# Down projections and pool mixer: which engine makes the token sums and one group's window average

## The chip, the cores and the metric

The kernel runs on one core of a Trainium2 chip. The metric is the device time of one execution in microseconds. All data are float32. TensorE is called PE, its weight loads PEld, VectorE is DVE, ScalarE is ACT, GpSimd is POOL, and SyncE (SP) issues most of the weight loads. Each engine takes its own instructions in the order in which they were written; semaphores tie the engines together.

## The reference, cut to what matters

Two blocks follow each other, each of depth 2, over 512 tokens and 1024 channels. The change touches the first block: the down projection of the gated feed-forward in both of its layers, and the pool mixer, which is the mixer of its second layer.

```python
def _pool_mixer(h, w_grp, scale):
    hf = h.reshape(Bn, T, POOL_GROUPS, POOL_GROUP)      # 4 groups of 256 channels
    for gi, w in enumerate((2, 4, 8, 16)):
        xg = hf[:, :, gi]
        cs = cumsum(pad(xg, w))                          # over the tokens
        outs.append((cs[:, w:] - cs[:, :T]) / minimum(t + 1, w) - xg)
    y = einsum('btgc,gcd->btgd', stack(outs), w_grp)
    return y.reshape(Bn, T, D) * scale

def _conv_ffn(h, w_up, conv_w, conv_b, w_down):
    u, v = split(h @ w_up)
    uc = conv_b + sum_j shifted(u, j) * conv_w[j]
    return (silu(uc) * v) @ w_down                       # depth 2816, 1024 outputs
...
    x = _layer_norm(ALPHA * x + g1 * y, ...)             # after the mixer
    x = _layer_norm(ALPHA * x + g2 * y, ...)             # after the feed-forward
```

## The kernel before

Data lie with channels on the partitions and tokens along the free dimension. The down projection multiplies `G` (22 depth tiles of 128 channels by 512 tokens) with `w_down`. It uses the seven-product form of a 2 by 2 block product: the two halves of the output channels are one pair, even and odd depth tiles the other, the two halves of the tokens the third. Four of the seven products need sums of weight blocks (**left sums**), four need sums of blocks of `G` (**token sums** or right sums, R[1] to R[4]).

The depth is cut in three groups, h = 0, 1, 2, with 4, 4 and 3 pairs of depth tiles. `DOWN` lists twelve steps (h, q), where q says which two output tiles are made: steps 0 to 3 are group 0, steps 4 and 5 group 1, steps 6 and 7 group 2, steps 8 and 9 group 1 again, steps 10 and 11 group 2. The token sums of a group are made once. A step has four parts on PE (`ffn_down_pe`, matmuls on L905): part 0 needs only the weights and `G`; part 1 is the first to need the left sums of the step and the token sums of the group.

Who does what in a step before the change:

- POOL (`ffn_pool`, `down_left_pool`) makes the left sums of each step, four tensor_tensor instructions (L823, L825, L826, L828), and right behind them issues the DMAs that bring tiles of `ada_rest` into three rotating buffers `ada_late`. The DMA of a tile waits until DVE has used the tile three places before ("ada used"). So the left sums of step it + 1 stand in POOL's queue behind DMAs that wait for DVE.
- DVE (`down_evac_dve`, L958 to L972) adds the seven products from PSUM into `R`, then makes two token sums or one (`down_right_dve`, L853 to L861), then works off the ada tiles of the step (`ada_tile_dve`, L350, or L354 and L357, each 128 x 1024). Four token sums of group 1 come one by one behind steps 0 to 3, those of group 2 in pairs behind steps 4 and 5.
- POOL makes the token sums of group 0 early, in the up projection (`first_right_pool`, L836 to L841).
- ACT copies the first product of a step out of PSUM.

In layer 1 DVE also has the sums of squares of the context behind step 0 and the context's normalisation (L1930) behind step 3. The buffer of R[4] of group 2 shares its place with the context's squares `ctx_sq`.

Behind the down projection of layer 0 comes a layer norm (`shifted_norm_dve`), then the pool mixer. DVE averages the groups of channels one after another (`pooled_dve`): group 0 (window 2) in the norm, then group 3 (window 16), group 2, and group 1 (window 4) last, all through the two buffers `pool_a` and `pool_b`, with the evacuations of finished rows between them (`pool_dve`). PE (`pool_pe`) takes the groups in the order 0, 3, 2, 1, with the matmuls against ones for the next norm between them. POOL has nothing to do there but to clear the pads (`pads_pool`).

Of the kernel before, what the change touches and what calls it, by code (L numbers as in the profile page):

```python
# [13 lines left out]
P = 128  # L14
D = 1024
DT = D // P
T = 512
# [362 lines left out]
def ffn_pool(k, l, first):  # L380

    def issued(until):
        nonlocal first
        last = min(until + LATE, N_ADA[0] + 96)
        late_tiles_pool(k, first, max(first, last))
        first = max(first, last)
    issued(ADA_UP[l][10].stop)
    first_right_pool(k, l)
    issued(ADA_UP[l][FT - 3].stop)
    for it in range(ND):  # L390
        down_left_pool(k, l, it)
        issued(ADA_UP[l][FT - 1].stop if it == 0 else ADA_DOWN[l][it - 1].stop)
    issued(ADA_DOWN[l][-1].stop)


# [445 lines left out]
    g.tensor_tensor(R[4], B[1, 0], R[2], ALU.subtract).then_inc(*k.says(POOL, "down right", l, 0))  # L841


def down_right_dve(k, l, h, j):

    v = k.nc.vector
    B, R = down_right(k, DOWN.index((h, 0)))
    if j == 0:
        if h == 1:
            v.wait_ge(*k.when("products", l, FT - 1, 3))  # L850
        else:
            v.wait_ge(*k.when("down products", l, 3, 3))
        v.tensor_tensor(R[1], B[0, 1], B[0, 0], ALU.subtract).then_inc(*k.says(DVE))  # L853
        v.wait_ge(*k.now(DVE))
    if j == 1:
        v.tensor_tensor(R[2], B[1, 1], R[1], ALU.subtract).then_inc(*k.says(DVE))
    if j == 2:
        v.tensor_tensor(R[3], B[1, 1], B[0, 1], ALU.subtract).then_inc(*k.says(DVE))
        v.wait_ge(*k.now(DVE))
    if j == 3:  # L860
        v.tensor_tensor(R[4], B[1, 0], R[2], ALU.subtract).then_inc(*k.says(DVE, "down right", l, h))  # L861


def ffn_down_pe(k, l):
# [113 lines left out]
def ffn_down_dve(k, l):  # L978
# [5 lines left out]
        v.tensor_tensor(sq[:, 0:2, :], sq[:, 0:2, :], sq[:, 4:6, :], ALU.add).then_inc(*k.says(DVE, st, "squares added"))  # L984
    for it in range(ND):
        down_evac_dve(k, l, it, squares_joined if it == ND - 1 else None)
        if it < 4:
            down_right_dve(k, l, 1, it)
        elif it == 4:
            for j in range(2):  # L990
                down_right_dve(k, l, 2, j)
        elif it == 5:
            for j in range(2, 4):
                down_right_dve(k, l, 2, j)
        if it == 7:
            v.tensor_tensor(sq[:, 0:2, :], R[:, 0:2, :], R[:, 2:4, :], ALU.add).then_inc(*k.says(DVE, st, "half"))
        if it == 8:
# [812 lines left out]
    g.wait_ge(*k.now(POOL))  # L1810


def pool_dve(k):

    v, st, rows = k.nc.vector, ("norm", 1, 0), ROWS["pool"]
    v.wait_ge(*k.when("pads"))
    pg = k.sc[:, 5, :]
    for n in range(DT):
        for g in ((3,), (), (2,), (), (1,), (), (), ())[n]:
            pooled_dve(k, g)  # L1820
        r = rows[n]
        v.wait_ge(*k.when("mm", "pool", 0, n))
        v.wait_ge(*k.when(("norm", 0, 1), "x", r))
        v.scalar_tensor_tensor(k.R[:, r, :], k.ps[:, n % 4, :], pg[:, r:r + 1], k.XA[:, r, :], ALU.mult, ALU.add)\
            .then_inc(*k.says(DVE, "evac", "pool", 0, n))
        if n == 5:
            v.wait_ge(*k.now(DVE))
            v.tensor_tensor(k.pool_a[:, 0, 0:T], k.R[:, 4, :], k.R[:, 5, :], ALU.add).then_inc(*k.says(DVE, "pool sum"))
            v.wait_ge(*k.when(st, "square", 5))
            v.tensor_tensor(k.pool_b[:, 0, 0:T], k.pool_sq[:, 4, :], k.pool_sq[:, 5, :], ALU.add).then_inc(*k.says(DVE, "pool square sum"))  # L1830
    k.mark(DVE, "pool rows")
    norm_scalars_dve(k, 1, 0)
    left_sums_dve(k, 1, 0)
    shifted_norm_dve(k, st)
# [1848 lines left out]
def lay_memory(k):  # L3683
# [59 lines left out]
    k.pool_a, k.pool_b = k.at("pool_a", [P, 2, T + PAD]), k.at("pool_b", [P, 2, T + PAD])  # L3743
    k.pooled = k.at("pooled", [P, DT, T])
    k.pool_sq = k.at("pool_sq", [P, DT, T])

    k.top = block2
    k.AR = [k.at("AR0", [P, 2, NK, 2, CK]), k.at("AR1", [P, 2, NK, 2, CK], xa)]
# [138 lines left out]
def gpsimd_program(k):  # L3887
# [8 lines left out]
        .then_inc(*k.lands("c2_rows_in", "c2 rows"))  # L3896
    ffn_pool(k, 0, N_EARLY)
    pads_pool(k)
    ffn_pool(k, 1, ADA_DOWN[0][-1].stop + LATE)
    rw_consts_pool(k)  # L3900
    end("pre 0")
# [113 lines left out]
```

## Time and profile before

| | |
|---|---|
| median of 3 runs | 2498.15 us (2493.9 to 2502.34) |
| profiled execution | 2495.48 us |
| its span | 2494.1 us, 39647 instructions |
| PE busy | 2334.1 us, 94% of the span |
| DVE busy | 1659.2 us, 67% |
| ACT busy | 640.2 us, 26% |
| POOL busy | 235.9 us, 9% |

The stages that matter here, in us from the span's start: the down projection of layer 0 runs from about 631 to 779, its norm and the pool mixer from 779 to 822, and the down projection of layer 1 from about 1099 to 1250.

A line of the timeline has the start, the length, the engine, the line of the kernel, the operation, what it writes and reads, and how many instructions are merged (xN). In square brackets is the idle time of the engine just before, and what ended it. Only idle time on the path that ends last costs anything.

### The profile page before, as it was taken

How to read it: one execution, taken by the hardware profiler on the slowest of the kernel's cores; microseconds unless marked ns; L12 is line 12 of the kernel's file. 1: busy time of each engine (PE TensorE's matmuls, PEld its weight loads, DVE VectorE, ACT ScalarE, POOL GpSimd, SP SyncE). 2: the span in 40 equal slices, each digit the busy share in tenths (PEclk: the TensorE clock that was granted, in tenths of full speed). 3: DMA queues.
4: the chain of work that ended last, by engine and by line, in shares of the span. 5: the costliest groups of instructions: out<-in, count | busy, mean ns of one | idle time of the engine just before them, and what ended most of it. 6: DMA issues, size and time to landing. Idle time of an engine off the chain costs nothing.

```text
span 2494.1 us, 39647 instructions
## 1 busy us (share of the span) xinstructions
PE 2334.1 (94%) x17066; PEld 1693.8 (68%) x17066; DVE 1659.2 (67%) x2800; ACT 640.2 (26%) x1314; POOL 235.9 (9%) x261
## 2 busy tenths in 40 slices
PE   7988889999997999999999999999997999999997
PEld 3675548888884688888756676676675654546973
DVE  3784378798799888879847879779787123232442
ACT  1323331111002311111043354444444212101111
POOL 2000000020541002024400000000000000000000
PEclk9999999999999999999999999999998999999999
DMA  8232135555432233343221101001010212111102
GB/s 329 90 113 76 60 134 169 172 170 181 161 131 89 85 128 126 135 139 132 95 98 70 40 19 35 21 20 37 3 36 19 85 51 84 51 52 66 35 18 101
DMA packets 42224, 227.99 MB, mean 91 GB/s; under 512 B 4737, under 2 KB 4865, under 8 KB 25793
## 3 DMA queue, kind: packets, MB, share of 16 engines
q1 hardware_dynamic: 21456, 140.56, 15.7%
q0 software_dynamic: 20016, 82.79, 9.8%
q8 instruction: 135, 2.21, 0.4%
q10 hardware_dynamic: 576, 2.11, 0.3%
q14 instruction: 41, 0.33, 0.0%
HBM read 219.14 MB, written 6.29 MB: 90 GB/s over the span
## 4 chain that ended last, share of the span: by engine, by line
PE 84%; DVE 11%; ACT 2%; issue 2%; DMA 1%; POOL 0%; SPq 0%; DVEq 0%; ACTq 0%; POOLq 0%
PE ps L683 20%; PE ps L2283 10%; PE ps L905 8%; PE ps L307 7%; PE ps L3383 3%; PE ps L2064 3%; PE ps L1039 3%; PE ps L455 2%; PE ps L1715 2%; PE ps L3572 2%; PE ps L2293 2%; PE ps L2302 2%; PE ps L3003 1%; PE ps L2971 1%; PE ps L2990 1%
## 5 line engine op out<-in xcount | busy, mean ns | idle before, releaser
L2283 PE MATMUL ps<-H,ring 128*128 128x256 f32 (+1 forms) x832 | 271.4, 487 | 5.4 <-ACT LW L2502 2.6
L683 PE MATMUL ps<-right_sums,left_sums 128*128 128x256 f32 x1056 | 242.8, 379 | 2.7 <-DVE left_sums L663 2.7
L2283 PEld LDWEIGHTS ps<-H,ring 128*128 128x128 f32 x832 | 157.4, 190 | 112.9 <-issue 92.8
L683 PEld LDWEIGHTS ps<-right_sums,left_sums 128*128 128x128 f32 x1056 | 200.5, 190 | 30.6 <-DVE left_sums L663 3.5
L307 PE MATMUL ps<-H,ring 128*128 128x512 f32 (+1 forms) x480 | 181.5, 535 | 0.9 <-DVE ls_tmp L3250 0.9
L683 PE MATMUL ps<-H,ring 128*128 128x256 f32 x704 | 164.2, 385 | 12.7 <-ACT H L626 12.7
L905 PE MATMUL ps<-G,ring 128*128 128x256 f32 x704 | 159.8, 379 | 0.0
L683 PEld LDWEIGHTS ps<-H,ring 128*128 128x128 f32 x704 | 134.6, 192 | 35.6 <-issue 12.8
L307 PEld LDWEIGHTS ps<-H,ring 128*128 128x128 f32 x480 | 91.1, 190 | 88.3 <-issue 84.9
L905 PEld LDWEIGHTS ps<-G,ring 128*128 128x128 f32 x704 | 133.8, 190 | 18.2
L377 POOL DMA_DIRECT2D ada_late<-ada_rest x104 | 56.2, 540 | 684.7 <-DVE mod L357 373.5
L750 ACT ACTIVATE C<-U,params_sb 128x512 f32<-128x512 f32 x44 | 35.9, 816 | 314.9 <-DVE U L775 314.9
L683 PE MATMUL ps<-H,left_sums 128*128 128x256 f32 x352 | 86.9, 388 | 0.0
L3383 PE MATMUL ps<-ring,H 128*128 128x256 f32 x384 | 85.9, 379 | 0.0
L2064 PE MATMUL ps<-O,ring 128*128 128x512 f32 (+1 forms) x256 | 83.6, 486 | 0.6 <-DVE H L2007 0.6
L683 PE MATMUL ps<-right_sums,ring 128*128 128x256 f32 x352 | 83.5, 379 | 0.0
L2007 DVE TENSOR_SCALAR H<-ps,scalars 128x512 f32<-128x512 f32 (+1 forms) x24 | 15.3, 661 | 97.7 <-ACT sq_ctx L2024 61.2
L3383 PEld LDWEIGHTS ps<-ring,H 128*128 128x128 f32 x384 | 72.0, 190 | 12.1 <-issue 3.1
L683 PEld LDWEIGHTS ps<-H,left_sums 128*128 128x128 f32 x352 | 68.2, 194 | 10.8 <-ACT H L626 1.4
L350 DVE CUSTOM_DVE_ANT_0 ada_late<-ada_late,c_row,params_sb 128x1024 f32<-128x1024 f32 x56 | 69.9, 1280 | 6.3 <-DMA ada_late<-ada_rest 6.2
L683 PEld LDWEIGHTS ps<-right_sums,ring 128*128 128x128 f32 x352 | 66.9, 190 | 9.1
L2064 PEld LDWEIGHTS ps<-O,ring 128*128 128x128 f32 x256 | 48.5, 190 | 34.0 <-issue 30.6
(593 smaller groups left out, 4704.2 us busy)
## 6 DMA issues: line engine op xcount, KB each, us to landing
ada_late<-ada_rest POOLq DMA_DIRECT2D x104, 512.0 KB, 3.7
ring<-w_up SPq DMA_DIRECT2D x44, 1024.0 KB, 4.8
ring<-w_down SPq DMA_DIRECT2D x16, 1024.0 KB, 4.9
ring<-od_in SPq DMA_DIRECT2D x16, 1024.0 KB, 4.8
ring<-ev_in SPq DMA_DIRECT2D x15, 1024.0 KB, 4.8
ada_early<-ada_rest POOLq DMA_DIRECT2D x24, 512.0 KB, 4.7
ada_first_sb<-ada_first SPq DMA_DIRECT2D x8, 1024.0 KB, 16.3
ring<-ab_in SPq DMA_DIRECT2D x7, 1024.0 KB, 6.4
```

The lines of the kernel that those rows point to most:

```text
L307: mm = pe.matmul(k.ps[:, (n % deep) * nb + b, 0:tn], wv[:, kk, a * P:(a + 1) * P], rhs[:, kk, t0:t0 + tn], start=(kk == 0), stop=(kk == kt ...
L350: v.tensor_tensor_reduce(w, w, k.c_row[:], 1.0, bias, ALU.mult, ALU.add, k.MOD[part][:, tile, :])\
L377: g.dma_start(k.late[:, j % LATE, :], k.dram["ada_rest"][j]).then_inc(*k.lands(f"late_in{j % LATE}", "ada in", j))
L455: mm = pe.matmul(k.ps[:, n, :], k.W8[:, kk, n * P:(n + 1) * P], k.H[:, kk, 0:T], start=(kk == 0), stop=(kk == DT - 1))
L683: return pe.matmul(product(k, n, j), lhsT[:, i, :], rhs[:, i, :], start=(i == 0), stop=(i == 3))
L905: mm = pe.matmul(product(k, it, j), left[:, i, :], right[:, i, :], start=(i == 0), stop=(i == ni - 1))
L1039: mm = pe.matmul(k.ps[:, bank, :], wv[:, kk, (i % 2) * P:(i % 2 + 1) * P], k.H[:, kk, 0:T], start=(kk == 0), stop=(kk == DT - 1))
L1715: return pe.matmul(out, wv[:, kk, (n % 2) * P:(n % 2 + 1) * P], rhs, start=start, stop=stop)
L2064: mm = k.nc.tensor.matmul(k.ps[:, 2 * (n % 2) + b, 0:tn], wv[:, kk, (n % 2) * P:(n % 2 + 1) * P], k.O[:, kk, t0:t0 + tn], start=(start and ...
L2283: mm = pe.matmul(k.ps[:, bank + b, 0:tn], wv[:, kk, (i % 2) * P:(i % 2 + 1) * P], k.H[:, kk, t0:t0 + tn], start=(kk == 0), stop=(kk == DT ...
L2293: mm = k.nc.tensor.matmul(k.ps[:, bank + n, 0:tn], lhsT, rhs[:, t0:t0 + tn], start=True, stop=True)
L3383: mm = pe.matmul(k.ps[:, 3 + 4 * (u % 2), 0:256], k.H[:, kk, t * P:(t + 1) * P], wv[:, kk, :], start=(kk == 0), stop=(kk == DT - 1))
```

## The change

DVE makes no token sums any more. POOL makes those of groups 1 and 2 too, in pairs: in steps 1 and 2 for group 1, in steps 4 and 5 for group 2. In POOL's queue they stand behind the left sums and the DMAs of the step, and ahead of the left sums of the next step. In layer 1 the first pair of group 2 waits in addition for the context's normalisation. In the pool mixer POOL averages group 1, in two buffers of its own (`pool_four`); it starts when the last tile of the norm is written, and its window average takes a tensor_scalar and a tensor_tensor where DVE used one scalar_tensor_tensor. DVE's `pool_dve` leaves group 1 out.

```diff
@@ ffn_pool
     for it in range(ND):
         down_left_pool(k, l, it)
         issued(ADA_UP[l][FT - 1].stop if it == 0 else ADA_DOWN[l][it - 1].stop)
+        if it in (1, 2):
+            down_right_pool(k, l, 1, it - 1)
+        if it in (4, 5):
+            down_right_pool(k, l, 2, it - 4)
@@
-def down_right_dve(k, l, h, j):
+def down_right_pool(k, l, h, j):
+    g = k.nc.gpsimd
     B, R = down_right(k, DOWN.index((h, 0)))
     if j == 0:
+        g.wait_ge(*k.when("ffn g", l, (7, 15, FT - 1)[h]))
+        g.wait_ge(*(k.when("products", l, FT - 1, 3) if h == 1 else k.when("down products", l, 3, 3)))
+        if h == 2 and l == 1:
+            g.wait_ge(*k.when("context normal", 1))
+        g.tensor_tensor(R[1], B[0, 1], B[0, 0], ALU.subtract).then_inc(*k.says(POOL))
+        g.wait_ge(*k.now(POOL))
+        g.tensor_tensor(R[2], B[1, 1], R[1], ALU.subtract).then_inc(*k.says(POOL))
+    else:
+        g.tensor_tensor(R[3], B[1, 1], B[0, 1], ALU.subtract).then_inc(*k.says(POOL))
+        g.wait_ge(*k.now(POOL))
+        g.tensor_tensor(R[4], B[1, 0], R[2], ALU.subtract).then_inc(*k.says(POOL, "down right", l, h))
@@ ffn_down_dve
         down_evac_dve(k, l, it, squares_joined if it == ND - 1 else None)
-        if it < 4:
-            down_right_dve(k, l, 1, it)
-        elif it == 4:
-            for j in range(2):
-                down_right_dve(k, l, 2, j)
-        elif it == 5:
-            for j in range(2, 4):
-                down_right_dve(k, l, 2, j)
@@
+def pooled_four_pool(k):
+    g, h, (src, dst) = k.nc.gpsimd, k.R[:, pair(1), :], k.pool_four
+    g.wait_ge(*k.when(("norm", 0, 1), "normal", 3))
+    for x in (src, dst):
+        g.memset(x[:, :, 0:PAD], 0.0).then_inc(*k.says(POOL))
+    g.tensor_scalar(src[:, :, PAD:PAD + 1], h[:, :, 0:1], 1.0, None, ALU.mult).then_inc(*k.says(POOL))
+    g.tensor_tensor(src[:, :, PAD + 1:], h[:, :, 1:], h[:, :, 0:T - 1], ALU.add).then_inc(*k.says(POOL))
+    g.wait_ge(*k.now(POOL))
+    g.tensor_tensor(dst[:, :, PAD:], src[:, :, PAD:], src[:, :, PAD - 2:PAD - 2 + T], ALU.add).then_inc(*k.says(POOL))
+    g.wait_ge(*k.now(POOL))
+    fix = k.f("pool_fix", 16, 16).unsqueeze(1).broadcast_to([P, 2, 16])
+    g.tensor_tensor(dst[:, :, PAD:PAD + 16], dst[:, :, PAD:PAD + 16], fix, ALU.mult).then_inc(*k.says(POOL))
+    g.wait_ge(*k.now(POOL))
+    g.tensor_scalar(dst[:, :, PAD:], dst[:, :, PAD:], 1.0 / POOL_WINDOWS[1], None, ALU.mult).then_inc(*k.says(POOL))
+    g.wait_ge(*k.now(POOL))
+    g.tensor_tensor(k.pooled[:, pair(1), :], dst[:, :, PAD:], h, ALU.subtract).then_inc(*k.says(POOL, "pooled", 1))
@@ pool_dve
-        for g in ((3,), (), (2,), (), (1,), (), (), ())[n]:
+        for g in ((3,), (), (2,), (), (), (), (), ())[n]:
             pooled_dve(k, g)
@@ gpsimd_program
     ffn_pool(k, 0, N_EARLY)
     pads_pool(k)
+    pooled_four_pool(k)
     ffn_pool(k, 1, ADA_DOWN[0][-1].stop + LATE)
```

## Rows read from the trace of the kernel before

**Rows 1.** The page: busy time of PE, and the chain's shares by engine.
```profile
PE 2334.1 (94%) x17066; PEld 1693.8 (68%) x17066; DVE 1659.2 (67%) x2800; ACT 640.2 (26%) x1314; POOL 235.9 (9%) x261
...
PE 84%; DVE 11%; ACT 2%; issue 2%; DMA 1%; POOL 0%; SPq 0%; DVEq 0%; ACTq 0%; POOLq 0%
```

**Rows 2.** Busy time in stretches: length, then PE, PEld, DVE, ACT, POOL, clock.
```profile
624.00:779.00 155.00, 149.40 (x671) 126.58 (x669) 130.21 (x202) 14.42 (x28) 71.73 (x69) 1.00 0.44 149
...
1092.00:1250.00 158.00, 150.96 (x671) 127.39 (x669) 134.08 (x193) 18.57 (x33) 72.58 (x61) 0.99 0.36 123
```

**Rows 3.** Timeline of PE, down projection of layer 0: the waits.
```profile
707.60 2.83 PE L905 MATMUL ps<-down_right,down_left 128*128 128x256 f32 x12 [1.03 <-DVE down_right_last L861]
...
718.33 2.86 PE L905 MATMUL ps<-down_right,down_left 128*128 128x256 f32 x12 [1.43 <-POOL ring L828]
...
771.92 1.98 PE L902 MATMUL ps<-H,consts_sb 128*128 128x512 f32 x4 [2.51 <-DVE H L984]
```

**Rows 4.** Timeline of PE, down projection of layer 1: parts 1 of steps 2, 5, 6, 7.
```profile
1126.92 3.62 PE L905 MATMUL ps<-down_right,down_left 128*128 128x256 f32 x16
...
1163.75 3.62 PE L905 MATMUL ps<-right_sums,down_left 128*128 128x256 f32 x16
...
1177.87 2.83 PE L905 MATMUL ps<-down_right,down_left 128*128 128x256 f32 x12 [2.73 <-DVE down_right_last L861]
...
1188.61 2.86 PE L905 MATMUL ps<-down_right,down_left 128*128 128x256 f32 x12 [1.44 <-POOL ring L828]
```

**Rows 5.** Timeline of PE, pool mixer: the first products of groups 0, 3 and 2.
```profile
787.61 5.20 PE L1871 MATMUL ps<-pooled,ring 128*128 128x512 f32 x8 [8.97 <-DVE pooled L1790]
797.84 5.22 PE L1871 MATMUL ps<-pooled,ring 128*128 128x512 f32 x8 [5.04 <-DVE pooled L1800]
...
806.33 3.60 PE L1871 MATMUL ps<-pooled,ring 128*128 128x512 f32 x8
```

**Rows 6.** Busy time in stretches, pool mixer behind that wait; columns as in rows 2.
```profile
803.10:822.00 18.90, 18.84 (x44) 7.98 (x42) 14.93 (x27) 3.95 (x7) 0.00 (x0) 1.00 0.16 55
```

**Rows 7.** Line L858: lengths of token sums on DVE, ns min/median/max.
```profile
L858 DVE TENSOR_TENSOR G<-G x4: 960/1226/1403, 669.0 to 1175.3; 128x1024 f32<-128x1024 f32 x2, 128x768 f32<-128x768 f32 x2
```

**Rows 8.** Timeline of POOL and of DVE: group 0's token sums beside left_sums.
```profile
502.53 2.37 POOL L836 TENSOR_TENSOR down_right<-G 128x1024 f32<-128x1024 f32 x1
...
505.38 2.83 DVE L661 TENSOR_TENSOR left_sums<-ring 128x512 f32<-128x512 f32 x1
508.25 2.72 DVE L662 TENSOR_TENSOR left_sums<-left_sums,ring 128x512 f32<-128x512 f32 x1
...
521.40 0.69 DVE L661 TENSOR_TENSOR left_sums<-ring 128x512 f32<-128x512 f32 x1
```

**Rows 9.** Timeline of POOL: the DMA right before the left sums of step 7, layer 0.
```profile
713.05 0.53 POOL L377 DMA_DIRECT2D ada_late<-ada_rest  x1 [2.19 <-PE ps L905]
```

**Rows 10.** Timeline of DVE: the ada tile before that DMA, a wait of step 1.
```profile
711.46 1.28 DVE L357 CUSTOM_DVE_ANT_0 ada_late<-ada_late,c_rows,params_sb 128x1024 f32<-128x1024 f32 x1
...
654.01 0.75 DVE L966 SCALAR_TENSOR_TENSOR R<-ps,mod,R 128x512 f32<-128x512 f32 x1 [1.11 <-PE ps L905]
```

**Rows 11.** Timeline of POOL, layer 1: last left sum of steps 2 and 5.
```profile
1125.33 1.27 POOL L828 TENSOR_TENSOR ring<-ring,down_left 128x512 f32<-128x512 f32 x1
...
1162.01 1.27 POOL L828 TENSOR_TENSOR ring<-ring,down_left 128x512 f32<-128x512 f32 x1
```

**Rows 12.** Timeline of DVE, pool mixer: group 3's second and last large instruction, group 2's last.
```profile
792.56 1.23 DVE L1795 TENSOR_TENSOR pool_b<-pool_a 128x1024 f32<-128x1024 f32 x1
...
796.57 1.22 DVE L1800 SCALAR_TENSOR_TENSOR pooled<-pool_b,R 128x1024 f32<-128x1024 f32 x1
...
803.22 1.23 DVE L1800 SCALAR_TENSOR_TENSOR pooled<-pool_a,R 128x1024 f32<-128x1024 f32 x1
```

**Rows 13.** Timeline of POOL and of DVE: a tensor_scalar on POOL beside DVE.
```profile
14.22 1.49 POOL L445 TENSOR_SCALAR XA<-XA 128x512 f32<-128x512 f32 x1 [13.77 <-ACT H L436]
...
14.76 1.28 DVE L424 CUSTOM_DVE_ANT_0 ada_first_sb<-ada_first_sb,c_row,params_sb 128x1024 f32<-128x1024 f32 x1 [1.54 <-DMA ab_first_sb<-ab_first]
```

More of the change, by code:

```diff
@@ L841, in first_right_pool @@
     g.tensor_tensor(R[4], B[1, 0], R[2], ALU.subtract).then_inc(*k.says(POOL, "down right", l, 0))
-def down_right_dve(k, l, h, j):
-    v = k.nc.vector
+def down_right_pool(k, l, h, j):
+    g = k.nc.gpsimd
     B, R = down_right(k, DOWN.index((h, 0)))
     if j == 0:
[L849 to L861, printed above, removed]
+        g.wait_ge(*k.when("ffn g", l, (7, 15, FT - 1)[h]))
[9 more added lines that the diff above has]
+        g.tensor_tensor(R[4], B[1, 0], R[2], ALU.subtract).then_inc(*k.says(POOL, "down right", l, h))
 def ffn_down_pe(k, l):
@@ L3745, in lay_memory @@
     k.pool_sq = k.at("pool_sq", [P, DT, T])
+    k.pool_four = [k.at(f"pool_four{n}", [P, 2, T + PAD]) for n in range(2)]
     k.top = block2
```

## The prediction

> **What bounds the kernel now.** I read the page first: PE is busy for 94% of the span and carries 84% of the chain that ended last [rows 1]. So work taken off DVE is worth only what a PE wait in front of it is worth. Next I read busy time by stretches: in both down projections PE is busy for 149.4 of 155 us and for 151.0 of 158 us [rows 2]. The two stages together cannot give more than some 12 us, and much of that lies behind other work. Then I read PE's timeline for waits. In layer 0 there are three that matter: 1.03 us for DVE's last token sum of group 2 (step 6), 1.43 us for POOL's left sums of step 7, and 2.51 us for a DVE sum of squares in step 11 [rows 3]. Layer 1 has the same pattern with 2.73 and 1.44 us in steps 6 and 7 [rows 4]. The change can touch the first two of each layer: 1.03 + 1.43 + 2.73 + 1.44 = 6.6 us is the most it can win there. In the pool mixer PE waits 5.04 us for group 3 from DVE [rows 5], and behind that wait it is busy for 18.84 of 18.90 us [rows 6]. Group 1, which moves to POOL, is averaged by DVE inside this dense stretch. It is hidden there, so taking it away gives PE nothing; but group 3, in front of it, is on the path.
>
> **The one cost that the change turns on: DVE beside POOL.** Up projection, group 0's token sums on POOL: one 128x1024 sum takes 2.37 us there. The DVE sums that run at the same time, 0.69 us long when alone, take 2.83 and 2.72 us [rows 8]. Their starts are 2.87 us apart. So a DVE instruction with two inputs in SBUF waits until POOL's sum has ended, and POOL's next sum then waits for DVE's. They alternate. One such wait costs DVE 2.72 - 0.69 = 2.03 us if DVE arrives when POOL starts, and less if it arrives later. I take 2.05 us for a 128x1024 sum, and 3/4 of it, 1.5 us, for the 128x768 sums of group 2. DVE saves 1.2 us for each token sum of 1024 and 0.96 us for one of 768 [rows 7]. Moving a sum therefore loses DVE time wherever DVE has a two-input instruction waiting, and gains where DVE works from PSUM or idles.
>
> **Layer 0, down projection.** POOL's pair in step 1 meets two ada tiles on DVE. DVE saves 1.2 and waits 0.8 (the rest of the first sum) and 2.05 (the second), so it is over 1.5 us late. DVE has idle time in step 1 (1.11 us before L966 alone [rows 10]), so it is back in step. The pair in step 2 again meets two ada tiles and adds some 2 us: two sums and two tiles in turn (about 2 x 2.1 + 2 x 1.1 us) now stand in POOL's queue where it had idle time before. The left sums of step 3 then come about 3.6 us later, which uses up the cover that they have; I book +0.5 us for PE. Group 2's sums are made in steps 4 and 5, in my count done by about 700, and PE wants them at 707.60 - 1.03 = 706.57 [rows 3], so the 1.03 us wait goes. What is late next are the left sums of step 7: POOL starts them right behind a DMA at 713.05 [rows 9], and that DMA waits until DVE has used the tile at 711.46 + 1.28 [rows 10]. The two token sums of 0.96 us that DVE made just before are gone, so the tile, the DMA, the left sums and PE's part 1 of step 7 move by -1.9 us. Of this 0.4 us is taken back by waits in steps 4 and 5. The sum is **-1.5 us** (bounds -1.9, where all contention falls in idle time, and 0). The later wait for DVE in step 11 stays at its size: PE and DVE both come 1.5 us earlier to it.
>
> Of the moved steps, DMAs count too. The ada DMAs stand in POOL's queue in front of the new sums of their own step, and those of the next step behind them. They are issued 1.5 to 3.6 us later than now, but always three tiles ahead, which is one step (8 to 12 us) or more; I book nothing for it. If that cover were gone, DVE would wait for tiles by the same 1.5 to 3.6 us.
>
> **Layer 1, down projection.** DVE is fuller here, as the sums of squares of the context come in step 0. The same pair delays DVE by 0.7 + 2.05 - 1.23 = 1.5 us and with it POOL's DMA and the left sums of step 2. These end at 1125.33 + 1.27 = 1126.60 [rows 11], and PE takes them at 1126.92 [rows 4], a slack of 0.3 us: PE waits 1.2 us more. In steps 2 to 4 another 0.8 us comes by the same way. In step 4 the first pair of group 2 waits for the context's normalisation on DVE. Queued behind that wait on POOL are the ada DMA and the left sums of step 5. Those end at 1163.28 now, 0.5 us before PE takes them at 1163.75 [rows 4, 11], and move by two sums less what overlaps, some 1.7 us: +1.2 us. At part 1 of step 6 the running total of about +3.2 us meets the 2.73 us wait that is no longer there, and at step 7 all is again set by DVE's ada tiles. In front of these DVE has lost two sums (1.40 and 0.96 us [rows 7], 2.4 us) and is itself between 2.7 and 4.0 us late. So PE's part 1 of step 7 lies between +0.3 and +1.6 us against 1188.61. I take **+1.0 us**; the bounds are -2.4 (no contention, DVE's two sums only) and +4.
>
> **Pool mixer.** POOL's chain starts when the norm's last tile is written, at the moment when DVE begins group 3, the instructions that PE waits for. These are five large ones of 1.2 us, all with two SBUF inputs; the second starts at 792.56, the last ends at 797.79 [rows 12]. POOL has three sums of 128x1024, one tensor_scalar of 128x1024, a few small ones. The first instruction of DVE (L1793) holds POOL up. Then they alternate: DVE's second and third large instruction each wait for one of POOL's sums, 2 x 2.05 = 4.1 us. Then comes POOL's tensor_scalar. The nearest row is one of 128x512, 1.49 us long from 14.22; a DVE instruction with two SBUF inputs that started at 14.76, inside it, kept its 1.28 us [rows 13]. So it holds DVE up for the first 0.54 us at most, and one of twice the size for about 1.1 us at most. I book 0.7 us. DVE then ends group 3 while POOL is still in its tensor_scalar (some 3 us, twice the 1.49), so POOL's last sum falls into group 2, which has 1.9 us of cover in PE's dense stretch (ready at 804.45 [rows 12], taken at 806.33 [rows 5]). The sum is **+4.8 us**; it adds to PE's wait of 5.04 us one for one, as PE is dense behind it. The bounds are 0 (nothing contends) and 9.2 (next part). POOL's result is there by about 807, while PE takes group 1 last, at about 818. The eight matmuls behind PE's wait take 5.22 us now, and those behind the 8.97 us of idle time before group 0 took 5.20 [rows 5], so a longer wait should not make them dearer.
>
> By the Trainium skill, page "SBUF — State Buffer", section "Who interferes with whom", the pair of ports that DVE and GpSimd share is an exclusive lock, held for the whole instruction. The trace agrees for sums [rows 8], but not for the tensor_scalar [rows 13]. By the page DVE would wait for the whole of it.
>
> **Sum.** -1.5 + 1.0 + 4.8 = +4.3 us. Against the profiled execution of 2495.48 us (span 2494.1) this gives 2499.8. That execution lies 2.7 us below the median of the runs shown, 2498.15; against the median the forecast is **2502.4 us**, 0.17% slower. A measurement of this kernel can tell about 0.3%, 7.5 us, from no change, so this is forecast as no measurable difference.
>
> **The rivals.**
> - **POOL's tensor_scalar holds DVE whole** (ends slower). Then DVE waits 3.0 us for it in place of 0.7, and POOL's last sum is in the queue before DVE's L1800 and costs 2.05 more: 4.1 + 3.0 + 2.1 = 9.2 us in the mixer, in all +8.7, 2506.9 us (0.35%). [rows 13] speak against it; what speaks for it is that the DVE instruction there began 0.54 us late and that no row has a 1024 one. It decides from a hold of about 2 us on. The page of the skill named above gives this result.
> - **POOL becomes the bound in the down projections.** The left sums behind the new pairs miss PE in steps 3 and 5 of layer 0 and in steps 2, 3, 5 and 6 of layer 1. With +4 in layer 1 and 0 in layer 0 this gives +8.8 us, 2507 us. The slacks of 0.3 and 0.5 us speak for it, DVE's relief and its idle time in layer 0 against it.
> - **Nothing contends.** If DVE's instructions slip between POOL's, the layers give -1.9 and -2.4 and the mixer 0: 2493.9 us. The alternation in [rows 8] speaks against it.
> - **The change doesn't do what it says**: POOL's chain in the mixer starts late (behind the DMAs in its queue) and meets group 2 instead. The mixer then gives 0, the layers -0.5: 2497.6 us.
>
> **How the numbers follow.** Forecast 0.57, tensor_scalar holding whole 0.17, POOL the bound 0.11, nothing contends 0.10, late chain 0.05. The forecast's own range is +0.5 to +7.5, 2498.6 to 2505.7. The range for 8 in 10 takes in the "nothing contends" case with the scatter of the runs and both slower rivals: 2494.5 to 2508.5. Faster by over 0.3% would need more than the 6.6 us that there are: 0.03. Slower by over 0.3% has about two thirds of the two slow rivals and the tail of the forecast: 0.20. The rest is 0.77.
>
> **What would show it.** In the changed profile: DVE's L1795 instructions of group 3 at about 3.3 us, each beside a POOL sum, and PE's wait for L1800 near 10 us in place of 5.04; POOL's tensor_scalar with DVE instructions of normal length inside it; no wait for a token sum at step 6 of layer 0; step 7's part 1 earlier by 1.5 us in layer 0, and new waits for L828 in steps 2 and 5 of layer 1. It would be wrong if L1795 keeps 1.23 us, if L1800 ends later than 804, or if PE's waits for L828 add up to more than 5 us in a layer.

## The result and the profile after

| | before | after |
|---|---|---|
| median of 5 runs | 2498.15 us (2493.9 to 2502.34) | 2512.07 us (2510.22 to 2516.36) |
| profiled execution | 2495.48 us | 2516.36 us |
| its span | 2494.1 us | 2515.1 us |
| down projection, layer 0 | 147.70 us | 153.30 us |
| norm and pool mixer | 43.00 us | 47.50 us |
| down projection, layer 1 | 151.99 us | 158.91 us |

The changed kernel takes 1.0057 times as long (95% interval 1.0046 to 1.0067), 13.9 us by the medians. The forecast was 2502.4 us and its range ended at 2508.5. The prediction was wrong: the change is slower, clear of the noise, and the loss is three times the sum of 4.3 us. In the trace the mixer's term came out. Both terms of the down projections did not.

The page after, busy time and the chain's shares (the lines of [rows 1]). DVE's busy time fell by 5.3 us only, POOL's rose by 51.9 us. POOL is now in the chain with 2%, where it had 0%.

```profile
PE 2343.7 (93%) x17066; PEld 1699.0 (68%) x17066; DVE 1653.9 (66%) x2779; ACT 638.8 (25%) x1314; POOL 287.8 (11%) x285
...
PE 82%; DVE 11%; POOL 2%; issue 2%; ACT 2%; DMA 1%; SPq 0%; DVEq 0%; POOLq 0%; ACTq 0%
```

Busy time in stretches, with the columns of [rows 2]: length, then PE, PEld, DVE, ACT, POOL, the granted clock (1.00 is 2.4 GHz, 0.50 is 1.2 GHz), the DMA share and GB/s. The stretches run from the first matmul of a down projection to its end, and from there to the end of the mixer. First the kernel before, as these cuts differ from those of [rows 2]:

```profile
631.30:779.00 147.70, 142.10 (x637) 120.16 (x635) 127.59 (x194) 13.60 (x27) 65.35 (x63) 1.00 0.46 156
779.00:822.00 43.00, 29.30 (x60) 12.52 (x60) 38.08 (x56) 13.17 (x20) 0.48 (x3) 0.88 0.11 39
1099.30:1251.29 151.99, 143.66 (x637) 121.00 (x636) 132.63 (x186) 18.20 (x32) 67.03 (x56) 0.99 0.38 131
```

Then the kernel after:

```profile
631.70:785.00 153.30, 145.96 (x637) 122.38 (x636) 125.16 (x186) 13.58 (x27) 83.75 (x71) 0.98 0.43 149
785.00:832.50 47.50, 30.19 (x60) 12.74 (x60) 40.10 (x51) 13.20 (x20) 13.84 (x11) 0.82 0.11 37
1109.90:1268.81 158.91, 145.71 (x638) 122.71 (x636) 128.26 (x178) 18.07 (x32) 86.83 (x64) 0.98 0.37 126
```

The three stages grew by 5.6, 4.5 and 6.9 us, 17.0 us in all. The two spans differ by 21.0 us, since this profiled execution lies 4.3 us above the median of its kernel and that of before 2.7 us below its own. Of the 4 us that the stages leave, 3.5 lie behind the second down projection, where the change touches nothing. The medians differ by 13.9 us only, so these two traces overstate the loss by some 3 us. Look at PE's columns too: for the same matmuls PE was busy 3.9 us longer in layer 0, and the clock column shows 0.98 in place of 1.00. So part of the loss is not waiting.

The timeline of PE after, for the stages of [rows 3], [rows 4] and [rows 5]:

```profile
673.74 5.41 PE L907 MATMUL ps<-down_right,down_left 128*128 128x256 f32 x16 [1.99 <-POOL ring L832]
...
701.86 5.41 PE L907 MATMUL ps<-right_sums,down_left 128*128 128x256 f32 x16 [1.99 <-POOL ring L832]
...
724.54 2.86 PE L907 MATMUL ps<-down_right,down_left 128*128 128x256 f32 x12 [0.44 <-POOL ring L832]
...
807.99 5.52 PE L1884 MATMUL ps<-pooled,ring 128*128 128x512 f32 x8 [8.41 <-DVE pooled L1794]
...
1141.45 5.41 PE L907 MATMUL ps<-down_right,down_left 128*128 128x256 f32 x16 [3.77 <-POOL ring L832]
...
1182.04 3.72 PE L907 MATMUL ps<-right_sums,down_left 128*128 128x256 f32 x16 [1.95 <-POOL ring L832]
...
1196.87 4.54 PE L907 MATMUL ps<-down_right,down_left 128*128 128x256 f32 x12 [3.33 <-POOL ring L832]
```

These are parts 1 of steps 3, 5 and 7 of layer 0, the mixer's group 3, and parts 1 of steps 2, 5 and 6 of layer 1. L832 is the last of POOL's left sums (L828 before), L1794 is DVE's L1800 of before. The waits for a token sum are gone, as forecast. In their place PE waits for POOL's left sums: 4.42 us in layer 0 and 9.05 us in layer 1, where these waits were 1.43 and 1.44 us. And behind four of the five long ones the next matmuls take 5.41 us for sixteen, in place of 3.62 us [rows 4], or 4.54 for twelve in place of 2.83.

Waits and slow matmuls account for the stages. Layer 0: waits 4.42 against 1.03 + 1.43 = 2.46, and 2 x 1.79 for slow matmuls, is +5.5 of 5.6 us. Layer 1: 9.05 against 2.73 + 1.44 = 4.17, slow matmuls 1.79 + 1.71 + 0.10, less 1.5 us that the kernel before lost in the same way near its end (shown under the experiments), is +7.0 of 6.9 us.

Why the left sums come late stands in POOL's timeline. First the kernel before, last DMA and left sums of step 3:

```profile
661.21 0.53 POOL L377 DMA_DIRECT2D ada_late<-ada_rest  x1 [0.64 <-DVE mod L350]
...
665.87 1.27 POOL L828 TENSOR_TENSOR ring<-ring,down_left 128x512 f32<-128x512 f32 x1
```

Then the kernel after: the same DMA, the second pair of token sums (L861, L863), and the left sums of step 3.

```profile
661.94 0.53 POOL L377 DMA_DIRECT2D ada_late<-ada_rest  x1 [0.64 <-DVE mod L350]
662.49 2.37 POOL L861 TENSOR_TENSOR G<-G 128x1024 f32<-128x1024 f32 x1
664.93 2.43 POOL L863 TENSOR_TENSOR right_sums<-G,right_sums 128x1024 f32<-128x1024 f32 x1
...
671.56 2.12 POOL L832 TENSOR_TENSOR ring<-ring,down_left 128x512 f32<-128x512 f32 x1
```

The DMA waits for DVE's ada tile and is issued 0.7 us later than before. The two sums are ready to run long before it, but stand behind it, so their whole 4.8 us come after it. The left sums end at 673.68 in place of 667.14, 6.5 us later, of which the last 0.9 us is a sum of 2.12 us beside a DVE instruction with two SBUF inputs. This second, smaller cause is there at other steps too. The four left sums of step 3 take 6.4 us from first start to last end, and took 5.4 before. In layer 1 they take 7.5 us in place of 5.7 at step 2 and 6.4 in place of 4.7 at step 6. PE wants them at 673.74 - 1.99 = 671.75.

### The profile page after: what moved, and what is told of

It reads as the page before. It is cut to its first block, busy times and chain, and to the rows that moved or that the text cites. A ratio compares the mean times of both kernels' runs of the same rounds, so it can differ in the third digit from the quotient of the medians.

```text
span 2515.1 us, 39651 instructions
## 1 busy us (share of the span) xinstructions
PE 2343.7 (93%) x17066; PEld 1699.0 (68%) x17066; DVE 1653.9 (66%) x2779; ACT 638.8 (25%) x1314; POOL 287.8 (11%) x285
## 4 chain that ended last, share of the span: by engine, by line
PE 82%; DVE 11%; POOL 2%; issue 2%; ACT 2%; DMA 1%; SPq 0%; DVEq 0%; POOLq 0%; ACTq 0%
PE ps L687 20%; PE ps L2296 10%; PE ps L307 7%; PE ps L907 5%; PE ps L3396 3%; PE ps L2077 3%; PE ps L1033 2%; PE ps L459 2%; PE ps L1709 2%; PE ps L3585 2%; PE ps L2306 2%; PE ps L2315 2%; PE ps L3016 1%; PE ps L2984 1%; PE ps L3003 1%
```

## The experiments

The theory after the result, **the queue**: the token sums are behind a DMA that waits for DVE, so their length lands whole on the left sums; the halved clock behind PE's waits multiplies it. The rivals: **the ports** (DVE and POOL hold each other up when both read SBUF, and DVE is late with its tiles), and **POOL's length alone** (the sums make POOL too slow wherever they stand). All ratios are against the kernel before on the same chip, with 95% intervals.

### One part at a time

Down projections only: the mixer of before, the rest as after.

```diff
-        for g in ((3,), (), (2,), (), (), (), (), ())[n]:
+        for g in ((3,), (), (2,), (), (1,), (), (), ())[n]:
@@
     pads_pool(k)
-    pooled_four_pool(k)
```

> The changed kernel with group 1 of the pool mixer back on DVE; the token sums stay on POOL. Theory (the two parts add up, each in its own stage, as the profiles read): the down projections keep their +5.6 us (layer 0) and +6.9 us (layer 1), the mixer returns to 43 us and PE's wait for group 3 to 5.0 us: +9 to +13 us against the kernel before. Rival (the mixer's delay hides or feeds waits of layer 1): the down projection of layer 1 comes back towards 152 us with it, and the total is +6 us or less.

Measured: 2508.48 us against 2497.11, ratio 1.0044 (1.0031 to 1.0057). PE's waits for L832 are 1.99, 2.00 and 0.45 us in layer 0, and 4.51, 1.96 and 1.38 us in layer 1. The +11.4 us lie in the range of +9 to +13 that was expected.

Pool mixer only: the kernel before with `pooled_four_pool` and its buffers.

```diff
+    k.pool_four = [k.at(f"pool_four{n}", [P, 2, T + PAD]) for n in range(2)]
@@
-        for g in ((3,), (), (2,), (), (1,), (), (), ())[n]:
+        for g in ((3,), (), (2,), (), (), (), (), ())[n]:
@@
     pads_pool(k)
+    pooled_four_pool(k)
```

> The kernel before with the mixer part of the change alone. Theory: DVE's instructions of group 3 alternate with POOL's, PE's wait for group 3 goes from 5.0 to about 9 us, nothing else moves: +4 to +4.5 us. Rival (what the prediction called nothing contends; the 4 us in the changed kernel came from the late down projection): 0.

Measured: 2499.81 against 2497.11, ratio 1.0011 (1.0002 to 1.0020). The two parts add to 0.55%, and both together gave 0.57%: no sign, within these intervals, that they help or hurt each other. The +2.7 us of the mixer are less than the +4 to +4.5 us that were expected. The timeline of PE in this run, group 3 again, and then busy time and clock in the stretch that follows (columns as above):

```profile
802.62 6.68 PE L1890 MATMUL ps<-pooled,ring 128*128 128x512 f32 x8 [8.96 <-DVE pooled L1800]
```

```profile
802.60:809.00 6.40, 6.38 (x8) 2.71 (x9) 6.30 (x6) 1.26 (x2) 2.98 (x2) 0.53 0.00 0
```

The wait is 3.9 us longer than in [rows 5], and here the eight matmuls run at a clock of 0.53 and take 6.68 us in place of 5.22. Mixer and norm grew by 5.4 us in this execution. The medians differ by 2.7 us only, so the trace shows where the time goes and not how much the runs lose.

### The order in POOL's queue

The changed kernel, token sums ahead of the DMAs of their step in POOL's queue; the same work, the same engines.

```diff
         down_left_pool(k, l, it)
-        issued(ADA_UP[l][FT - 1].stop if it == 0 else ADA_DOWN[l][it - 1].stop)
         if it in (1, 2):
             down_right_pool(k, l, 1, it - 1)
         if it in (4, 5):
             down_right_pool(k, l, 2, it - 4)
+        issued(ADA_UP[l][FT - 1].stop if it == 0 else ADA_DOWN[l][it - 1].stop)
```

> The changed kernel with one thing moved: in POOL's queue the token sums of a step stand ahead of the ada DMAs of the step in place of behind them. Theory (the cost in the down projections is the queue order: the sums start only when DVE has used its ada tiles, and the left sums of the next step are late by that): PE's waits of 1.99 us at steps 3 and 5 of layer 0 shrink to 0.5 us or less, the stage of layer 0 goes from 153.3 to about 147, layer 1 from 158.9 to about 153; in all 8 to 12 us faster than the changed kernel, +2 to +6 against before. Rival (the port that DVE and POOL share is what costs): the sums run beside the ada tiles instead and DVE is slowed as much; the stages stay within 2 us of 153.3 and 158.9.

Measured: 2501.44 against 2497.11, ratio 1.0017 (1.0008 to 1.0026), +4.3 us. The changed kernel had 1.0057, so the order of two calls gives back 0.40%, some 10 us, of the 0.44% that the down projections cost; the mixer's cost stays. From the first product to the last, layer 0 takes 146.2 us, where the kernel before took 146.3. Layer 1 takes 150.5 in place of 149.5, and its waits for left sums are 0.81, 1.95 and 1.38 us at steps 5, 6 and 7, 4.1 us in place of 9.05. The timeline of POOL and of DVE, step 1, then POOL's last left sum of step 3:

```profile
642.93 2.80 POOL L857 TENSOR_TENSOR right_sums<-G 128x1024 f32<-128x1024 f32 x1
645.81 3.21 POOL L859 TENSOR_TENSOR right_sums<-G,right_sums 128x1024 f32<-128x1024 f32 x1
...
668.56 1.26 POOL L832 TENSOR_TENSOR ring<-ring,down_left 128x512 f32<-128x512 f32 x1
```

```profile
644.86 1.95 DVE L350 CUSTOM_DVE_ANT_0 ada_late<-ada_late,c_row,params_sb 128x1024 f32<-128x1024 f32 x1
```

Here the sums do meet DVE's tiles: the sums take 2.80 and 3.21 us in place of the 2.37 and 2.36 that they took in the changed kernel, and a tile 1.95 in place of 1.28; the next tile takes 3.36. Over the down projection of layer 0 DVE is busy for 131.1 us here and for 124.9 in the changed kernel, with the same instructions, and in layer 1 for 134.6 and 126.7. So there is more contention than in the changed kernel, and less time lost. That speaks against **the ports** as the cause of the loss. They keep a share in it: in the changed kernel the left sums, pushed back by the order, are slowed by the tiles that they then meet, as told above. In the changed kernel the step's second tile was over at 647.92, before the first sum began at 648.77 (DVE, then POOL):

```profile
646.64 1.28 DVE L350 CUSTOM_DVE_ANT_0 ada_late<-ada_late,c_row,params_sb 128x1024 f32<-128x1024 f32 x1
```

```profile
648.23 0.53 POOL L377 DMA_DIRECT2D ada_late<-ada_rest  x1 [0.64 <-DVE mod L350]
648.77 2.37 POOL L857 TENSOR_TENSOR right_sums<-G 128x1024 f32<-128x1024 f32 x1
```

It speaks against **POOL's length alone** as well: the left sums of step 3 now end at 669.82, in front of PE.

### Four matmuls in front of the wait

The changed kernel with four extra matmuls on PE, with a result that nobody reads, before the wait for the left sums in steps 3 and 5 of layer 0 and 2 and 6 of layer 1. Idle time becomes work of no use; no other instruction is changed.

```diff
         for e, terms in enumerate(steps):
+            if e == 1 and (l, it) in ((0, 3), (0, 5), (1, 2), (1, 6)):
+                for _ in range(4):
+                    pe.matmul(k.ps[:, 4 * (it % 2) + 3, HALF:T], A[0, 0][:, 0, :], B[0, 0][:, 0, :], start=True, stop=True)
             if e == 1:
                 pe.wait_ge(*k.when("down left", l, it))
```

> The changed kernel with four more matmuls (128x128 by 128x256, into a PSUM half that nobody reads, 1.7 us of PE time) just ahead of the wait for the left sums in steps 3 and 5 of layer 0 and 2 and 6 of layer 1. They are work beyond the reference and their results are not used. Theory (PE's clock falls to half behind such a wait because PE was idle, 1.8 us on top of the wait): in layer 0, where the waits are 1.99 us, the first matmuls behind the wait take 3.6 us in place of 5.4, the stage goes from 152 to about 148.5 us; in layer 1 the waits were 3.8 and 3.3 us and 2 us of idle time stay, so less certain; in all -3 to -6 us against the changed kernel. Rival (the fall has another cause, such as the load that came before): no change in the stage's length.

Measured: 2505.66 against 2497.70, ratio 1.0034 (1.0022 to 1.0045). The changed kernel had 1.0057, so more work on PE made it about 0.23%, some 6 us, faster. PE in this run, steps 3 and 5 of layer 0 with extra matmuls, step 2 of layer 1 with them, and step 5 of layer 1 without:

```profile
671.43 3.72 PE L910 MATMUL ps<-down_right,down_left 128*128 128x256 f32 x16 [0.18 <-POOL ring L832]
...
697.87 3.72 PE L910 MATMUL ps<-right_sums,down_left 128*128 128x256 f32 x16 [0.27 <-POOL ring L832]
...
1136.61 5.41 PE L910 MATMUL ps<-down_right,down_left 128*128 128x256 f32 x16 [2.80 <-POOL ring L832]
...
1177.22 5.41 PE L910 MATMUL ps<-right_sums,down_left 128*128 128x256 f32 x16 [1.96 <-POOL ring L832]
```

Where the idle time in front is filled, the matmuls behind it keep their length of full clock; where 2.80 or 1.96 us stay, they don't. At steps 3 and 5 of layer 0 they were slow in both kernels without the filler (the changed one and the one with the down projections only), so this is hardly chance. The slow matmuls need PE's idle time in front of them; what POOL and the DMAs do at that moment is not enough. It accounts for 2 x 1.79 us in layer 0. The rest of the 6 us is not taken apart here: the wait at step 6 of layer 1 is gone too, while step 5 of layer 1, at full clock in the changed kernel, is slow here.

### The mixer without the overlap

The mixer-only kernel, but POOL waits until DVE has ended group 3.

```diff
-    g.wait_ge(*k.when(("norm", 0, 1), "normal", 3))
+    g.wait_ge(*k.when("pooled", 3))
```

> The kernel before with the mixer part alone, but POOL starts on group 1 only when DVE has finished group 3. Theory (the mixer's cost is POOL's sums in turn with DVE's group 3, in front of PE's wait, and group 1 has no worth on either engine): PE's wait for group 3 is back at 5.0 us, DVE's group 2 is slowed instead and has 1.9 us of cover; the stage is that of before plus 0 to 2 us, in all 0 to +2 us. Rival (freeing DVE of group 1 is worth something once the wait is gone): 1 us or more faster than before.

Measured: 2498.47 against 2497.70, ratio 1.0003 (0.9995 to 1.0012). PE, groups 3 and 2, then POOL's tensor_scalar, then DVE beside it:

```profile
797.60 5.40 PE L1890 MATMUL ps<-pooled,ring 128*128 128x512 f32 x8 [4.34 <-DVE pooled L1800]
...
807.52 3.70 PE L1890 MATMUL ps<-pooled,ring 128*128 128x512 f32 x8 [1.09 <-DVE pooled L1800]
```

```profile
804.19 3.70 POOL L1827 TENSOR_SCALAR pool_four<-pool_four 128x1024 f32<-128x1024 f32 x1
```

```profile
805.29 0.91 DVE L1799 TENSOR_TENSOR pool_a<-pool_a,first_consts_sb 128x32 f32<-128x32 f32 x1
806.24 1.23 DVE L1800 SCALAR_TENSOR_TENSOR pooled<-pool_a,R 128x1024 f32<-128x1024 f32 x1
```

The long wait is gone and no loss can be measured; a new wait of 1.09 us for group 2 takes its place. The traces show that POOL's sums beside DVE's group 3 make the long wait: it is 8.96 us with them and 4.34 us without. The run times alone don't separate the two mixers, +2.7 and +0.8 us with intervals that overlap. There is no gain from group 1 leaving DVE either, even with group 3 undisturbed.

### Less on POOL, in another order

Group 1 stays on DVE as before, group 2's sums are made by POOL ahead of the DMAs, and only the one sum whose buffer needs it waits for the context.

```diff
         down_left_pool(k, l, it)
+        if it in (4, 5):
+            down_right_pool(k, l, 2, it - 4)
         issued(ADA_UP[l][FT - 1].stop if it == 0 else ADA_DOWN[l][it - 1].stop)
```

> The kernel before, with the token sums of group 2 alone on POOL, ahead of the ada DMAs of steps 4 and 5; the wait for the context's normalisation stands only before R[4], whose buffer needs it. Group 1 stays on DVE, and so does the whole mixer. Theory: these eight sums fit in idle time of POOL; the waits of 1.03 and 2.73 us at step 6 go and the left sums of step 7 come earlier: -2 us in layer 0, -2 us in layer 1, about -4 us in all. Rival (port): DVE loses in steps 4 and 5 what it saves, the time is that of before within 1 us.

Measured: 2494.29 against 2497.11, ratio 0.9993 (0.9984 to 1.0002): no difference that can be measured, where about -4 us was expected. The two stages together take 1.4 us less in the trace, about what the kernel before lost to slow matmuls at the end of layer 1 and this one did not (1.5 us, shown in the last part). PE's waits for left sums are 0.98 and 0.89 us in layer 0, and 1.01, 1.96 and 1.73 in layer 1. They are waits behind a DMA still, now at steps 5 to 7. I tried three ways to be rid of them, and all three missed. First, the left sums of step 7 ahead of the DMAs behind step 6 too:

```diff
             down_right_pool(k, l, 2, it - 4)
+        if it == 6:
+            continue
```

> The kernel before, with group 2's token sums on POOL ahead of the ada DMAs (as in e4) and with the left sums of step 7 ahead of the DMAs that wait for DVE's two ada tiles of step 5. Theory (what is late at step 7 is POOL's wait for DVE in front of a DMA): the wait for left sums at step 7 (0.9 and 1.7 us in e4) goes; about -5 us against before. Rival (the left sums of step 7 are bound by something else, such as the slab's arrival or the products of step 5): as e4, -2.5 us.

Measured: 2499.22 against 2497.70, ratio 1.0010 (1.0001 to 1.0019). Second, the DMAs of steps 4 to 6 one step behind:

```diff
-        issued(ADA_UP[l][FT - 1].stop if it == 0 else ADA_DOWN[l][it - 1].stop)
+        issued(ADA_UP[l][FT - 1].stop if it == 0 else ADA_DOWN[l][it - (2 if it in (4, 5, 6) else 1)].stop)
```

> As e4 (group 2's token sums on POOL, the rest as before), and in steps 4, 5 and 6 POOL issues the DMAs only as far as the tiles that DVE used one step earlier, so that no left sums stand behind a wait for DVE. Theory (queue order): all waits for left sums in steps 5, 6 and 7 (0.98 and 0.89 us in layer 0, 1.01, 1.96 and 1.73 in layer 1 of e4) go, about -6 us against before, unless the tiles now come late for DVE. Rival (the tiles come late, DVE becomes the bound): DVE waits for ada_late and the time is that of e4 or worse.

Measured: 2505.19 against 2497.70, ratio 1.0038 (1.0024 to 1.0051). PE's wait at step 7 of layer 1 is gone in both (that of 1.96 us at step 6 stays in the first and goes in the second), and a longer one stands one step further on. Step 8 of layer 1, first the kernel with the left sums ahead:

```profile
1198.02 5.41 PE L927 MATMUL ps<-right_sums,down_left 128*128 128x256 f32 x16 [2.48 <-POOL ring L832]
```

then the one with the late DMAs:

```profile
1202.81 6.75 PE L925 MATMUL ps<-right_sums,down_left 128*128 128x256 f32 x16 [5.82 <-POOL ring L830]
```

A DMA that is put off still waits for DVE's tile, and the left sums that come behind it have a shorter way to their matmuls than before. The wait is pushed along the queue and grows. Third, group 2's sums on POOL as in the first kernel of this part, and the steps in which DVE works off two ada tiles moved: of steps 3 and 5 to 2 and 4 in layer 0, of 4 and 5 to 2 and 7 in layer 1 (`ADA_DOWN`, which DVE's tiles and POOL's DMAs both follow; of its two lines only the changed part is shown):

```diff
-... (0, 2), (2, 4), (4, 5), (5, 7), (7, 8), (8, 10), (10, 11), ...
+... (0, 2), (2, 4), (4, 6), (6, 7), (7, 9), (9, 10), (10, 11), ...
@@
-... (0, 1), (1, 2), (2, 3), (3, 4), (4, 6), (6, 8), (8, 9), (9, 10), ...
+... (0, 1), (1, 2), (2, 4), (4, 5), (5, 6), (6, 7), (7, 8), (8, 10), ...
```

> As e4 (group 2's token sums on POOL ahead of the DMAs, the rest as before), and the steps behind which DVE works off two ada tiles are moved: from steps 3 and 5 to steps 2 and 4 in layer 0, from steps 4 and 5 to steps 2 and 7 in layer 1. Theory (each left-sum wait of e4 stands behind the DMA of the second tile of the step two before it): the waits at steps 5 and 7 of layer 0 (0.98 and 0.89 us) and at steps 6 and 7 of layer 1 (1.96 and 1.73 us) go, 5.5 us beyond e4, about -7 to -8 us against before. Rival (as in e8 and e9 the wait only moves to a later step): within 1 us of e4, that is -2 us.

Measured: 2497.95 against 2500.15, ratio 0.9995 (0.9986 to 1.0004). The waits moved once more: 1.92 us at step 6 of layer 0, 2.52 us at step 5 of layer 1. And the same change of `ADA_DOWN` alone, on the kernel before, with all of DVE's token sums on DVE:

> The kernel before with the ada tiles moved as in e10 and nothing else; all token sums of groups 1 and 2 stay on DVE. Theory: DVE is late at steps 5 and 6 as before, mostly by its own token sums, but the waits for left sums at step 7 go, and the wait for DVE's last token sum shrinks where DVE has one tile less in front of it: -2 to -4 us. If it is as fast as e10, the token sums on POOL are worth nothing and the timing of the tiles is all.

Measured: 2493.94 against 2500.15, ratio 0.9982 (0.9973 to 0.9991). It is the only kernel here whose interval lies below 1. It is faster than before by 6.2 us or 0.18%, more than the -2 to -4 us expected, though by less than the 0.3% that I count as a difference. The waits of PE for the left sums of steps 2 to 7 are gone; what it waits for now is again DVE:

```profile
707.85 2.83 PE L905 MATMUL ps<-down_right,down_left 128*128 128x256 f32 x12 [1.74 <-DVE down_right_last L861]
...
1175.48 2.83 PE L905 MATMUL ps<-down_right,down_left 128*128 128x256 f32 x12 [0.64 <-DVE down_right_last L861]
```

With the same steps for the tiles, POOL's token sums of group 2 give 0.9995 and DVE's 0.9982. So even in the better order there is no sign of a gain in having POOL make them.

### The clock behind a wait

Two kernels, the same step (step 5 of layer 1), the same wait (1.96 and 1.95 us), and the clock behind it. Down projections only, then the changed kernel:

```profile
1175.40:1177.40 2.00, 0.04 (x2) 0.01 (x1) 1.97 (x3) 0.37 (x1) 1.93 (x1) 1.00 0.13 52
1177.40:1181.00 3.60, 3.60 (x11) 2.96 (x12) 3.42 (x5) 0.00 (x0) 0.57 (x1) 0.65 0.27 97
```

```profile
1180.10:1182.00 1.90, 0.00 (x0) 0.00 (x0) 1.86 (x3) 0.37 (x1) 1.89 (x1) 1.00 0.08 32
1182.00:1185.70 3.70, 3.66 (x17) 3.25 (x18) 3.52 (x5) 0.00 (x0) 0.57 (x1) 1.00 0.26 76
```

PE stood still in both. Behind it the one had a mean clock of 0.65, 11 matmuls in 3.6 us, the other of 1.00, 17 in 3.7. The same pair exists at the end of layer 1, this time to the bad of the kernel before. Before, then after:

```profile
1241.63 3.47 PE L902 MATMUL ps<-H,consts_sb 128*128 128x512 f32 x4 [2.70 <-DVE H L984]
```

```profile
1260.64 1.98 PE L904 MATMUL ps<-H,consts_sb 128*128 128x512 f32 x4 [2.69 <-DVE H L986]
```

A wait of 2 to 3 us can thus cost 1.5 to 1.8 us on top of itself, or nothing. What decides it is open.

## Why the prediction was wrong

**What bounds the kernel, and the 6.6 us.** Not contradicted: the best arrangement tried, tiles moved and no sum on POOL, took 2.1 us off the two stages in its trace and 6.2 us off the median.

**DVE beside POOL.** The alternation was right where it happened: in the mixer two large instructions of DVE take 2.79 and 2.80 us beside POOL's. They are the third and fourth of group 3 and not the second and third; the second kept its 1.22 us. Each lost 1.57 us and not the 2.05 that I took. They began 1.24 and 1.04 us behind the POOL sum that they waited for (rows below), so less of it was left.

**Layer 0, -1.5 forecast, +5.6 measured.** The step that failed is "POOL's pair in step 1 meets two ada tiles on DVE", and with it "now stand in POOL's queue where it had idle time before". The paragraph on the DMAs says itself that they stand in front of the new sums. The DMA waits for DVE's tile, so the sums can't begin before the tiles are done, and POOL's idle time in front of the DMA is of no use to them: in the changed kernel they begin at 648.77, behind the tile that ended at 647.92. I had counted them as if they ran in POOL's idle time, as they do in the run with the sums first. For that order the sum came out, +4.3 us by the medians and +4.3 forecast, but in part by luck: in its trace layer 0 lies at -0.2 us for a term of -1.5, layer 1 at +1.0 for +1.0, and norm and mixer at +5.4 for +4.8. For the real order the left sums of step 3 came 6.5 us later and not 3.6, against a cover of 671.01 - 667.14 = 3.9 us. The 1.9 us that I expected at step 7 was there in part (a wait of 0.44 in place of 1.43), but behind two new waits of 1.99.

**Layer 1, +1.0 forecast, +6.9 measured.** The same step, three times. At step 2 the left sums end at 1141.39 where 1126.60 plus the 10.6 us by which the stage begins later would be 1137.2: 4.2 us late for a slack of 0.3, where I had 1.5. Some 2.5 us of it come from the later start of the left sums and 1.7 from their greater length beside DVE's tiles, for which I had no term. At step 5 I had 1.2 us and PE waits 1.95. At step 6, where I expected the vanished wait to pay the total back, stand two DMAs that wait for DVE's tiles and then a pair of sums. POOL after:

```profile
1186.14 0.53 POOL L377 DMA_DIRECT2D ada_late<-ada_rest  x1 [2.20 <-DVE mod L357]
1186.69 1.82 POOL L861 TENSOR_TENSOR G<-G 128x768 f32<-128x768 f32 x1
...
1194.95 1.85 POOL L832 TENSOR_TENSOR ring<-ring,down_left 128x384 f32<-128x384 f32 x1
```

The last left sum takes 1.85 us there, beside a tile on DVE, where the same instruction took 1.00 us in the kernel before, and PE waits 3.33 us.

**The clock.** It had no term at all. The sentence that a longer wait should not make the matmuls behind it dearer rested on two waits of the mixer [rows 5] and failed: +1.8 us behind each of three waits in the down projections and +1.7 behind a fourth, 7 us in all, or 5.6 us net of the 1.5 us that the kernel before lost in this way. The two stages lost 12.5 us together. The page's clock column in [rows 2], 1.00 and 0.99, was no warning, since there were few waits there to show it. But [rows 5] itself was one: the eight matmuls behind both waits take 5.2 us, and the same eight of group 2, behind no wait, 3.60. Both rows were slow already, so they could not show that a wait is free of this cost. The kernel before has it in its second down projection too, 3.47 us for four matmuls (shown above) where layer 0 has 1.98 [rows 3].

**Pool mixer, +4.8 forecast, +4.5 measured.** Right in size in this trace, and nearly in its parts: 2 x 1.57 us for the two sums, where I had 2 x 2.05, and 0.83 us for the tensor_scalar, where I had 0.7, 4.0 us in all. Here are DVE and POOL after, from the third large instruction of group 3 on:

```profile
800.00 2.79 DVE L1789 TENSOR_TENSOR pool_a<-pool_b 128x1024 f32<-128x1024 f32 x1
802.83 2.80 DVE L1789 TENSOR_TENSOR pool_b<-pool_a 128x1024 f32<-128x1024 f32 x1
...
805.88 2.05 DVE L1794 SCALAR_TENSOR_TENSOR pooled<-pool_b,R 128x1024 f32<-128x1024 f32 x1
```

```profile
798.76 2.95 POOL L1814 TENSOR_TENSOR pool_four<-R 128x1022 f32<-128x1022 f32 x1
801.79 2.75 POOL L1816 TENSOR_TENSOR pool_four<-pool_four 128x1024 f32<-128x1024 f32 x1
...
805.81 2.77 POOL L1821 TENSOR_SCALAR pool_four<-pool_four 128x1024 f32<-128x1024 f32 x1
```

PE's first products of group 3 come 14.20 us behind those of group 0, 10.23 us before: these are DVE's 4.0 us. The wait shows 3.4 of them (5.04 to 8.41), since the products of group 0 in front of it took 5.78 us in place of 5.20 and filled the rest. The matmuls behind the wait add 0.3 us. By the medians the mixer alone costs 2.7 us (0.5 to 5.0 by the interval), so the size of the forecast is at the upper end of what the runs allow.

**The rivals.** "POOL becomes the bound in the down projections" is what happened, in five of the six steps that it named. It had a chance of 0.11 and a price of 8.8 us, because I gave it 0 in layer 0, on the strength of an idle time of DVE that has nothing to do with a queue on POOL. "Holds DVE whole" is false: DVE's L1794 began at 805.88, 0.07 us behind POOL's tensor_scalar, and ended at 807.93, inside it, as that lasted until 808.58; in the run without the overlap one of 1.23 us ran inside a tensor_scalar of 3.70 us. "Nothing contends" and "doesn't do what it says" are false by the rows above. My own sign for a wrong prediction, waits for the left sums of more than 5 us in a layer, is met in layer 1 with 9.05.

## What to carry to other kernels

When an instruction is moved to an in-order queue, ask not whether that engine has idle time but on which side of its next wait the instruction stands: idle time in front of a wait is worth nothing to what is behind it. Work out the arrival of everything that is queued behind the moved work against the time at which it is needed, step by step, and price a new wait of 2 us on PE at up to twice its length: here it cost 1.8 us more in some cases and nothing in others. And before giving work to another engine, look at the timing of what both wait for; here the two lists of steps for the ada tiles gave the only gain beyond the noise, and the sums on POOL gave none.

## What the runs showed of the hardware

- **A wait of PE for some 2 us can be followed by a stretch at half the clock.** The granted clock was 1.00 during the wait, and behind it sixteen matmuls of 128x256 took 5.41 us in place of 3.62, at a mean clock of 0.65 in the stretch shown; in the mixer it was 0.53 behind 8.96 us. A wait as long at the same step left the clock at 1.00 in another kernel, so the length alone doesn't decide it.
- **The ports.** POOL's tensor_scalar of 128x1024 held a DVE instruction with two SBUF inputs up by 0.8 us only, though it lasts 2.77 us. The Trainium skill, page "SBUF — State Buffer", section "Who interferes with whom", calls the pair of ports that DVE and GpSimd share an exclusive lock; of DVE's 2-port modes it says that whoever issues first has the pair for the whole instruction. The sums of 128x1024 agree with such a lock (2.79 and 2.80 us on DVE in place of 1.23), the tensor_scalar does not.
